# Rotary partner rows on VectorE by a shuffle instead of on TensorE by a matmul, interleaved with the attention units

## What is computed

```
h = RMSNorm(x);  proj = h @ w_in
x += concat(window attention, HGRN2, short gated conv)(proj) @ w_out
x += SwiGLU(RMSNorm(x))
```

```
def partial_rope(x, pos):
    half = ROT_DIM // 2                       # 8
    x1, x2 = xr[..., :half], xr[..., half:]   # xr: the first 16
    rot = concatenate([x1 * cos - x2 * sin, x2 * cos + x1 * sin], axis=-1)
    return concatenate([rot, x[..., ROT_DIM:]], axis=-1)
```

## Time and profile before

| | |
|---|---|
| median of 3 runs | 2613.02 us (2607.78 to 2615.09) |
| profiled execution, its own time | 2616.4 us |
| span of the profiled execution | 2614.8 us |
| TensorE (PE) busy | 2576.7 us, 99% |
| VectorE (DVE) busy | 1484.4 us, 57% |
| ScalarE (ACT) busy | 1015.0 us, 39% |
| GpSimd (POOL) busy | 344.1 us, 13% |
| granted TensorE clock, mean | 0.992 |

### The profile page before, as it was taken

One profiled execution on the slowest core, in us unless ns is written; L12 is line 12 of the kernel. 1 busy time (PEld: TensorE's weight loads), 2 busy tenths in 40 slices (PEclk: granted clock), 3 DMA queues, 4 the chain that ended last, 5 costly groups with the idle time before them and its releaser, 6 DMA issues.

```text
span 2614.8 us, 51520 instructions
## 1 busy us (share of the span) xinstructions
PE 2576.7 (99%) x19424; PEld 2536.5 (97%) x19424; DVE 1484.4 (57%) x2054; ACT 1015.0 (39%) x1409; POOL 344.1 (13%) x285
## 2 busy tenths in 40 slices
PE   8999999999999999999999999999999999999997
PEld 8999999999999999999999999999999999999997
DVE  5467787555554455555555776875555444555555
ACT  5344554433333333333333535543333333333333
POOL 2011113111110011111100111131111000111111
PEclk9999999999999999999999999999999999999998
DMA  6445444544455544544454444444444545444543
GB/s 224 154 139 170 149 141 145 172 163 163 160 169 161 167 155 166 171 161 167 160 161 156 166 147 141 141 161 161 160 162 167 177 153 173 161 163 160 169 161 124
DMA packets 115724, 419.97 MB, mean 161 GB/s; under 512 B 13376, under 2 KB 14656, under 8 KB 115584
## 3 DMA queue, kind: packets, MB, share of 16 engines
q1 hardware_dynamic: 109152, 397.72, 45.8%
q0 software_dynamic: 3472, 14.04, 1.5%
q10 hardware_dynamic: 3024, 7.16, 0.7%
HBM read 411.06 MB, written 11.87 MB: 162 GB/s over the span
## 4 chain that ended last, share of the span: by engine, by line
PE 96%; DVE 2%; POOL 1%; ACT 1%; issue 0%; DMA 0%; DVEq 0%; SPq 0%; ACTq 0%; POOLq 0%
PE gp L1424 31%; PE gp L1426 30%; PE gp L1425 30%; PE mb L1468 1%; PE mb L1579 1%; PE mb L1600 0%; PE mb L1592 0%; POOL acc L1352 0%; PE mb L1477 0%; PE mb L1567 0%; PE mb L1538 0%; DVE rstd L724 0%; PE mb L1634 0%; DVE wlo L699 0%; DMA raw<-wstream 0%
## 5 line engine op out<-in xcount | busy, mean ns | idle before, releaser
L1424 PE MATMUL gp<-xh,whi 128*128 128x288 f32 x4096 | 1228.2, 300 | 12.9 <-DVE xl L1123 9.8
L1425 PE MATMUL gp<-xl,whi 128*128 128x288 f32 x4096 | 1211.9, 296 | 0.0
L1426 PE MATMUL gp<-xh,wlo 128*128 128x288 f32 x4096 | 1208.0, 295 | 0.0
L699 DVE TENSOR_TENSOR wlo<-raw,whi 128x1024 fp32r<-128x1024 f32 x754 | 971.1, 1322 | 345.6 <-ACT whi L410 342.0
L410 ACT ACTIVATE whi<-raw 128x1024 fp32r<-128x1024 f32 x754 | 769.0, 1052 | 578.6 <-PE gp L1426 539.7
L1424 PEld LDWEIGHTS gp<-xh,whi 128*128 128x128 f32 x4096 | 771.5, 188 | 25.1 <-issue 24.1
L1426 PEld LDWEIGHTS gp<-xh,wlo 128*128 128x128 f32 x4096 | 774.5, 189 | 0.0
L1425 PEld LDWEIGHTS gp<-xl,whi 128*128 128x128 f32 x4096 | 772.6, 189 | 0.9
L1424 PE MATMUL gp<-fh,whi 128*128 128x288 f32 x1408 | 416.7, 296 | 0.0
L1425 PE MATMUL gp<-fl,whi 128*128 128x288 f32 x1408 | 415.4, 295 | 0.0
L1426 PE MATMUL gp<-fh,wlo 128*128 128x288 f32 x1408 | 414.0, 294 | 0.0
(11 more groups left out here) (249 smaller groups left out, 1868.1 us busy)
## 6 DMA issues: line engine op xcount, KB each, us to landing
raw<-wstream SPq DMA_DIRECT2D x754, 512.0 KB, 4.2
s<-s_cache POOLq DMA_DIRECT2D x8, 512.0 KB, 9.8
hs_out<-s ACTq DMA_DIRECT2D x8, 512.0 KB, 2.8
caches_out<-caches POOLq DMA_DIRECT2D x8, 496.0 KB, 8.0
x<-x_in ACTq DMA_DIRECT2D x4, 576.0 KB, 8.7
y_out<-x SPq DMA_DIRECT2D x4, 576.0 KB, 2.8
kct<-kt_cache POOLq DMA_DIRECT2D x4, 512.0 KB, 6.5
vct<-v_cache POOLq DMA_DIRECT2D x4, 512.0 KB, 7.2
```

The costliest lines, as they stand in the source:

```text
L699: v.tensor_tensor(wlo[slot][:], raw[slot][:], whi[slot][:].bitcast(F32), ALU.subtract).then_inc(lo_ready, 1)
L1424: t.matmul(out, w_hi, mv_hi, start=first, stop=False)
L1425: t.matmul(out, w_hi, mv_lo, start=False, stop=False)
L1426: mm = t.matmul(out, w_lo, mv_hi, start=False, stop=last)
```

## The change

The partner is no longer made by a matmul. VectorE multiplies the projected tile by the sine table first, then swaps partner rows with one shuffle inside each quadrant of 32 partitions (in place), then adds the product by cosine as before. The sign of the partner (minus for the first half) is put into the sine table once, in `half_masks` of the first layer, by two instructions. TensorE's five partner matmuls of each trip are gone, with two of its slots' contents: `score(0)` stands in f2 and waits for `rot0` alone (and `krx`), f3 is empty, and `score(u)` waits for `rot{u}`. VectorE's tiles are spread: f1 `rope` 4 and 0; f2 `scores(0)` and `rope` 1; f3 `rope` 2 and `probs(0)`; f4 `rope` 3; f5 `scores(1)` as before. ScalarE's order becomes f2 `krx`, f3 `exps(0)`, f4 `kvt` and then `qs`, which still waits for `rot3`. GpSimd's cache loads now follow `rot4`, though in its queue they still stand behind the last product by `cos`, which waits for `rot1`. The diff, without the semaphore lists:

```
+PARTNER = [(i ^ (ROT_DIM // 2)) if i < ROT_DIM else i for i in range(32)]
...
@@ half_masks (VectorE)
+                if l == 0:
+                    v.tensor_reduce(rot_sign[:], rot, AX.X, ALU.add).then_inc(signs_made, 1)
+                    v.wait_ge(signs_made, 1)
+                    apart(v)
+                    v.tensor_scalar(sin, sin, rot_sign[:, 0:1], None, ALU.mult).then_inc(signs_made, 1)
+                    v.wait_ge(signs_made, 2)
@@ attn (VectorE)
                 def rope(n):
                     k = ROPE_ORDER.index(n)
-                    v.wait_ge(at.sem, at.at(T, f"R{n}"))
-                    v.tensor_tensor(rs_a[:, k % 2, :], mb[k % 4][:, 0:TOK], sin, ALU.mult
-                                    ).then_inc(av.sem, av.step(f"sin{n}"))
+                    tile = 4 * gg + Q0 + n if n < 4 else gg + KV
+                    v.tensor_tensor(rs_a[:, k % 2, :], pj[:, tile, :], sin, ALU.mult).then_inc(av.sem, av.step(f"sin{n}"))
                     v.wait_ge(av.sem, av.at(T, f"sin{n}"))
+                    v.stream_shuffle(rs_a[:, k % 2, :], rs_a[:, k % 2, :], PARTNER).then_inc(av.sem, av.step(f"shf{n}"))
+                    v.wait_ge(av.sem, av.at(T, f"shf{n}"))
                     v.wait_ge(ap_.sem, ap_.at(T, f"cos{n}"))
                     v.tensor_tensor(krg[:] if n == 4 else qg[:, n, :], rs_a[:, k % 2, :], rt_a[:, k % 2, :], ALU.add
...
-                for n in ROPE_ORDER[:4]:
+                v.wait_ge(group_out, attn_in(l))
+                for n in ROPE_ORDER[:2]:
                     rope(n)
-                yield
-                rope(ROPE_ORDER[4])
...
                 yield
                 scores(0)
-                yield
+                rope(1)
+                yield
+                rope(2)
                 probs(0)
+                yield
+                rope(3)
                 yield
                 scores(1)
@@ attn (ScalarE)
                 a.activation(krx[64:128, :], krg[0:64, :], ACT.Copy).then_inc(aa.sem, aa.step("krx"))
                 yield
+                exps(0)
+                yield
+                a.wait_ge(at.sem, at.at(T, "tv"))
+                a.activation(kvt[:], mb[2][:, 0:2 * P].rearrange("p (m e) -> p m e", m=2), ACT.Copy)
+                a.activation(vnt[:], mb[3][0:SAMP, 0:P], ACT.Copy).then_inc(aa.sem, aa.step("kvt"))
                 a.wait_ge(av.sem, av.at(T, "rot3"))
...
                 m.then_inc(aa.sem, aa.step("qs"))
-                yield
-                exps(0)
-                a.wait_ge(at.sem, at.at(T, "tv"))
-                a.activation(kvt[:], mb[2][:, 0:2 * P].rearrange("p (m e) -> p m e", m=2), ACT.Copy)
-                a.activation(vnt[:], mb[3][0:SAMP, 0:P], ACT.Copy).then_inc(aa.sem, aa.step("kvt"))
                 yield
@@ attn (GpSimd)
-                e.wait_ge(av.sem, av.at(T, f"rot{ROPE_ORDER[-1]}"))
+                e.wait_ge(av.sem, av.at(T, "rot4"))
@@ conv (VectorE and GpSimd)
-                v.wait_ge(at.sem, at.at(T * 2 + 1, "R3"))
+                v.wait_ge(av.sem, av.at(T * 2 + 1, "rot3"))
@@ attn (TensorE)
-                    t.wait_ge(av.sem, av.at(T, f"sc{u - 1}" if u else "rot3"))
+                    t.wait_ge(av.sem, av.at(T, f"sc{u - 1}" if u else "rot0"))
                     if u == 0:
                         t.wait_ge(aa.sem, aa.at(T, "krx"))
+                    else:
+                        t.wait_ge(av.sem, av.at(T, f"rot{u}"))
...
-                for n in ROPE_ORDER[:4]:
-                    partners(n)
-                yield
-                t.wait_ge(av.sem, av.at(T, f"sin{ROPE_ORDER[0]}"))
-                partners(ROPE_ORDER[4])
                 yield
                 score(0)
                 yield
+                yield
                 t.wait_ge(ap_.sem, ap_.at(T, "vst"))
```

More of the change, by code:

```diff
@@ L161, in build @@
         qz = sb("qz", [P, DEC_BATCH, SAMP])
+        rot_sign = sb("rot_sign", [P, 1])
         half_mask = {i: sb(f"half_mask{i}", [P, P // (2 * HALVES[i])]) for i in MASKED}
@@ L321, in build @@
                                         "norm"])
+        signs_made = sem("signs_of_sines_made")
         masks_made = sem("half_masks_made")
@@ L329, in build @@
         c_store = sem("conv_buffer_stored")
-        av = Steps(sem("attn_vector"), [s for n in ROPE_ORDER for s in (f"sin{n}", f"rot{n}")]
[1 row of a table removed]
+        av = Steps(sem("attn_vector"), [f"{s}{n}" for n in ROPE_ORDER[:2] for s in ("sin", "shf", "rot")]
+                   + ["sc0", "mx0", "mm0", "nm0", "ds0"]
+                   + [f"{s}{n}" for n in ROPE_ORDER[2:4] for s in ("sin", "shf", "rot")]
[1 row of a table added]
                    + ["sc1", "mx1", "mm1", "nm1", "ds1", "den1", "rec1", "p1", "al0"]
@@ L335, in build @@
                    + ["ssn", "smx", "smm", "snm", "sds", "sden", "srec", "sp", "asb", "sal"])
-        aa = Steps(sem("attn_scalar"), ["krx", "qs", "es0", "kvt", "pT0", "es1", "ah0", "pT1", "es2", "ah1", "pT2", "es3", "ah2",
+        aa = Steps(sem("attn_scalar"), ["krx", "es0", "kvt", "qs", "pT0", "es1", "ah0", "pT1", "es2", "ah1", "pT2", "es3", "ah2",
                                         "pT3", "ah3", "sst", "ses", "pts", "sah"])
         ap_ = Steps(sem("attn_gpsimd"), [f"cos{n}" for n in ROPE_ORDER] + ["vst", "stored"])
-        at = Steps(sem("attn_tensor"), [f"R{n}" for n in ROPE_ORDER]
-                   + ["sc0", "tv", "sc1", "pt0", "pv0", "sc2", "pt1", "pv1", "sc3", "pt2", "pv2", "pt3", "pv3"]
+        at = Steps(sem("attn_tensor"), ["sc0", "tv", "sc1", "pt0", "pv0", "sc2", "pt1", "pv1", "sc3", "pt2", "pv2", "pt3", "pv3"]
                    + ["st", "ss", "pts", "pvs"])
@@ L1286, in conv @@
             def conv(T):
-                e.wait_ge(at.sem, at.at(T * 2 + 1, "R3"))
+                e.wait_ge(av.sem, av.at(T * 2 + 1, "rot3"))
                 e.wait_ge(ap_.sem, ap_.at(T * 2 + 1, "vst"))
```

## The result

The changed kernel took 2618.83 us (median of 8 runs, 2615.89 to 2620.60), the kernel before 2611.92 us (8 runs, 2607.76 to 2616.19). The ratio is 1.0027 with an interval of [1.0016, 1.0037]: 6.9 us slower, 4.2 to 9.7. The forecast was 8.8. The loss is real, since its interval leaves out 1, and it lies just under the 0.3% that the prediction took for the least that could be told from no change. Of the 3.0 us between 2618.8 and the forecast 2621.8, 1.1 is the kernel before, whose median was 2613.0 when the forecast was made.

The account below looks back on a forecast made before the run. TensorE, busy 2576.7 of 2614.8 us, was taken as the bound, with its stalls. Trips 0 and 2 lose 1.2 us each, 1 and 3 lose 3.2: 8.8 slower, 2613.0 + 8.8 = 2621.8 us, range 2608 to 2632.

Parts of the forecast that it names:

- The terms: VectorE's ropes: shuffle 0.45 us, rope about 1.35; product waits about 0.45 for GpSimd; `score(0)` waits 2.5 and 1.2.
- halfway case: VectorE's new products don't wait for GpSimd: 3.6 us slower, 2616.6 us; chance 0.12.
- The chain: Late `rot3` delays `qs`, `hi`, seventh `lo`: trip 1 ends 3.2 us later, trip 0 1.2.
- Rival 1: Seventh slab's late `hi` is absorbed, only `score(0)` costs: 2.4 us faster, 2610.6 us; chance 0.28.
- rival 3: All that TensorE sheds comes through: 10.5 us gained, 2602.5 us; chance 0.04.
- The step that missed: Trip 0, `turn(1)`: TensorE gets there at 294.5 and waits 1.3 us.
- Rival 2: VectorE's shuffle permutation is written by its own instruction every time, 0.16 us each: 3.2 us more, 2625.0; chance 0.16.
- The wait of 0.3 us at `tv`: In f4 `tv` waits some 0.3 us for GpSimd's value copy, behind the cosine product that waits for `rot1`.

Follow-up runs that it names:

- e1: The changed kernel with ScalarE's sample queries (`qs`) moved from f4 to behind `turned(1)`: 2615.35 us, ratio to before 1.0013.
- e5: e1 with the convolution's slots on VectorE and ScalarE one later: 2609.23 us, ratio to before 0.9993.
- e11: The changed kernel with only ropes 4 and 0 moved ahead of the `lo` of slot f1 on VectorE: 2617.83 us, ratio to before 1.0028.
- e8: The kernel before the change with the convolution's slots alone one later: 2610.12 us, ratio to before 1.0002.
- 0-stretch line: Second line of the trip-length table: nearly the order of the kernel before, no low-clock stretch in a trip, ratio to before 1.0002.
- e7: e6 with the attention's first slot (ropes 4 and 0) ahead of the first `lo` on VectorE: 2603.46 us, ratio to before 0.9975.
- e6: e5 with ropes 1, 2, 3 in f3, f5, f7, `qs` behind `turned(2)`, GpSimd's value copy ahead of its third product: 2609.32 us, ratio to before 0.9998.
- e2: The changed kernel's shuffle rope in the slot order of the kernel before, `score(0)` in f3 behind `rot3`: 2622.49 us, ratio to before 1.0041.
- e3: The changed kernel with three shuffles in each rope instead of one, values unchanged: 2641.56 us, ratio to before 1.0117.
- e4: The changed kernel's slot order with partners still by matmul, four in f1 and tile 3's in f4: 2615.27 us, ratio to before 1.0013.

## Why the prediction was right

**The terms.** Shuffle 0.47 us against 0.45 assumed, a rope 1.37 (271.90 to 273.27) against 1.35. The product does contend with GpSimd: 1.06 us beside the pair against 0.45, which rules out the halfway case at 2616.6. The Trainium skill (SBUF — State Buffer, Who interferes with whom) has the two exclude each other; these rows agree. `rot0` in trip 0 was forecast for 273.25 and `score(0)` started at 273.41, in a trip that itself started 0.27 us later; the waits were 2.29 and 1.00 us against 2.5 and 1.2.

**The chain.** In trip 1: `rot3` forecast 355.4, ended 355.47; `hi` 358.3, ended 358.50; the seventh `lo` 3.2 us late, measured 3.43 (358.53 against 355.10); `turn(3)` at 385.76 against 382.34, 3.42 late; 0.10 of each is the trip's own later start. In trip 0: `lo` 288.15 forecast, 288.50 measured; the end of `out_lo(0)` 295.75 forecast, 296.11 measured, 0.27 of each being the trip's own later start:

```profile
295.69 0.42 DVE L1014 TENSOR_TENSOR ml<-mb,mh 128x256 fp32r<-128x256 f32 x1
```

e1, e5 and e11 show by intervention what was argued: move `qs`, and half of the loss goes; take 1.8 us of convolution out of the way of `out_lo(2)`, and the rest of `turn(3)`'s wait goes, while the same move in the kernel before changes nothing (e8); shorten the wait before `score(0)` alone, and nothing goes. Rival 1 (a late `hi` absorbed, 2610.6) and rival 3 (all 10.5 us gained) fall with it.

**The step that missed.** "it gets there at 273.25 + 17.7 + 3.2 + 0.3 = 294.5 and waits 1.3", of TensorE at `turn(1)` of trip 0: it waited 0.28, because it came at 295.9, held back by a low-clock stretch that stands in no step of mine. The end of the trip was right all the same (1.34 against 1.2), since VectorE sets it. For the same reason the sum of the trips, 9.8 us against the 0-stretch line, is more than the 6.9 of the medians: in the kernel before each stretch costs 1.5 to 1.7 us in full, in the changed one some fall where TensorE would wait. That this makes up the 3 us is argued from the table, not shown; outside the trips the two profiles differ by only 0.6 us (2326.1 and 2326.7). The trips came out 1.0 us above the forecast loss and the medians 1.9 below it, both by the clock at least in part, for which the prediction has no term: that the median lies so close is to that extent luck.

**Rival 2** was half true: the mask load is issued at every shuffle, as the condition had it (the Trainium skill, Vector Engine (DVE) Microarchitecture Reference, section 3.8, describes it as an instruction of its own). But it takes 0.01 us, not 0.16: 0.2 us in all instead of 3.2.

The wait of 0.3 us at `tv` did not show in the changed kernel (TensorE came late to it), but did in e11, at up to 1.4.

## What to carry to other kernels

Taking work off the bottleneck engine pays only if what it waits for comes no later: 10 us left TensorE, 9 us went to VectorE just where VectorE was 88 to 93% busy, and half of the loss hung on a copy on a third engine (`qs`) that nobody needed for another 30 us (it ended at 287.4 in trip 0, the cache scores started at 318.1), queued ahead of one that everybody needed. Look, in each queue, at what stands behind the instruction that waits for the slowed work, and move out of the way what has a late consumer, before moving the score itself sooner: the same edit gave 0 before such moves (e11) and 5.9 us after them (e7). And compare profiles by stretches at equal granted clock: here one low-clock stretch more or less is worth as much as the effect sought.

## What the runs showed that was not expected

A short stand of TensorE was often followed by time at the lower clock. In all five profiles where it stood 2.3 us before `score(0)` in trips 0 and 2 (changed kernel twice, e1, e5, e6: ten trips) a stretch of 3.4 us at the 1.2 GHz level followed, from between 0.1 us before the score's start and 1.7 us after it. In e7 and e11, with 0.6 to 0.8 us of standing (four trips), none did, nor behind the ten stands of 1.0 us in trips 1 and 3 of those five profiles. In trips 0 and 2 of e2 and e3, with 4.3 to 4.6 us, the stretch lasted 6.8 us.

But the length of the stand alone does not decide it. In trips 1 and 3 of e2 and e3 TensorE stood 3.1 to 3.3 us before `score(0)`, longer than 2.3, and a stretch followed in two of the four. Trip 3 of e2 has none:

```profile
1642.55 0.37 PE L1583 MATMUL mb<-krg,qg 64*128 64x128 f32 x1 [3.32 <-DVE qg L962]
```

```profile
1642.00:1650.00 8.00, 7.45 (x58) 7.11 (x59) 6.87 (x17) 5.92 (x21) 1.77 (x4) 1.00 0.84 310
```

Of the eighteen stands of 1.75 to 1.93 us at a `turn` (changed kernel twice, e1, e3, e4, e11), seven were followed by a stretch. And the stretches of before behind the small cache-score matmuls at 318 and 390 follow no stand at all; such stretches moved from kernel to kernel and are missing in e7 and e8, which issue the same matmuls there. What decides is open, and so is whether the stand is the cause in trips 0 and 2.
